# A two-layer decoder step on one core: each weight block multiplied in five matmuls instead of six, the tokens split 286/234 instead of 260/260

## The reference, cut to what matters

```
h = h + rmsnorm(mixer(rmsnorm(h)))
u = rmsnorm(h) @ w_up                     # 1024 x 5632
c = conv_b + u[t-2]*w0 + u[t-1]*w1 + u[t]*w2
h = h + rmsnorm((silu(c[:2816]) * c[2816:]) @ w_down)
h = h + sigmoid(rmsnorm(h) @ w_gate) * (p @ w_proj)
```

## Time and profile before

| | |
|---|---|
| median of 3 runs | 1551.48 us (1548.21 to 1552.59) |
| span of the profiled execution | 1546.4 us, 27972 instructions |
| matmul instructions | 11049, of which 9648 in `product` |
| TensorE busy | 93% of the span |
| VectorE busy | 59% |
| ScalarE busy | 33% |
| DMA | 129.91 MB, mean 84 GB/s |

### The profile page before, as it was taken

The page is one execution under the profiler, slowest core; times in us unless marked ns, Lnnn a source line. Parts: engine busy times, 40 slices in busy tenths (PEclk is TensorE's granted clock), DMA queues, the critical chain, the costliest instruction groups (busy, mean ns, idle before and its releaser), DMA issues.

```text
span 1546.4 us, 27972 instructions
## 1 busy us (share of the span) xinstructions
PE 1433.8 (93%) x11049; PEld 1353.1 (88%) x11049; DVE 909.3 (59%) x1457; ACT 507.8 (33%) x804; POOL 79.6 (5%) x85
## 2 busy tenths in 40 slices
PE   6989998979999999999698988896999999999797
PEld 6989854869999999999698966696999999999787
DVE  4345443568777776322885565747777777522473
ACT  5121130234443443222422134624434434311241
POOL 2000100020000000000400010003000000000110
PEclk9999999889999999999899987998999999999899
DMA  6222510112222223222322220021222222322211
GB/s 206 95 68 84 202 69 14 61 60 69 84 92 95 89 87 111 91 93 90 115 82 71 78 86 1 1 82 32 91 95 83 93 95 89 111 94 93 82 51 72
DMA packets 32643, 129.91 MB, mean 84 GB/s; under 512 B 3961, under 2 KB 4049, under 8 KB 32065
## 3 DMA queue, kind: packets, MB, share of 16 engines
q1 hardware_dynamic: 27792, 110.36, 21.9%
q0 software_dynamic: 4800, 18.86, 3.5%
HBM read 120.57 MB, written 10.04 MB: 84 GB/s over the span
## 4 chain that ended last, share of the span: by engine, by line
PE 85%; DVE 9%; ACT 2%; POOL 2%; issue 2%; DMA 0%; SPq 0%; ACTq 0%; DVEq 0%
PE tile L689 74%; POOL h L357 2%; PE side L729 2%; PE side L862 1%; PE side L959 1%; DVE sm L1532 1%; PE sums L714 1%; DVE cg L1064 1%; PE sums L801 1%; DVE xL L1068 1%; DVE soft L1547 1%; DVE pxL L1068 1%; DVE cv L1079 1%; PE tile L864 1%; PE tile L847 1%
## 5 line engine op out<-in xcount | busy, mean ns | idle before, releaser
L689 PE MATMUL tile<-xH,wH 128*128 128x260 f32 x2256 | 465.1, 287 | 39.9 <-DVE xL L1068 36.1
L455 ACT ACTIVATE wH<-raw 128x1024 fp32r<-128x1024 f32 (+2 forms) x189 | 214.0, 1132 | 766.9 <-PE tile L689 710.9
L689 PE MATMUL tile<-xH,wL 128*128 128x260 f32 x2256 | 457.1, 284 | 0.0
L689 PE MATMUL tile<-xL,wH 128*128 128x260 f32 x2256 | 456.4, 284 | 0.0
L689 PEld LDWEIGHTS tile<-xH,wH 128*128 128x128 f32 x2256 | 352.9, 190 | 49.9 <-issue 37.5
L689 PEld LDWEIGHTS tile<-xH,wL 128*128 128x128 f32 x2256 | 350.3, 190 | 0.0
L689 PEld LDWEIGHTS tile<-xL,wH 128*128 128x128 f32 x2256 | 349.7, 190 | 0.0
L1038 DVE TENSOR_TENSOR wL<-raw,wH 128x1024 fp32r<-128x1024 f32 (+2 forms) x189 | 248.5, 1315 | 162.0 <-ACT wH L455 161.3
L689 PE MATMUL tile<-hidH,wH 128*128 128x260 f32 x704 | 142.1, 283 | 0.1
L689 PE MATMUL tile<-hidH,wL 128*128 128x260 f32 x704 | 141.5, 282 | 0.0
L689 PE MATMUL tile<-hidL,wH 128*128 128x260 f32 x704 | 141.4, 282 | 0.0
(11 more groups left out here) (264 smaller groups left out, 1553.5 us busy)
## 6 DMA issues: line engine op xcount, KB each, us to landing
raw<-in_w_up SPq DMA_DIRECT2D x88, 512.0 KB, 3.3
raw<-in_w_down SPq DMA_DIRECT2D x32, 704.0 KB, 4.0
raw<-in_w_ple SPq DMA_DIRECT2D x16, 640.0 KB, 4.0
raw<-in_w_kv SPq DMA_DIRECT2D x13, 512.0 KB, 3.4
raw<-in_w_qo SPq DMA_DIRECT2D x12, 512.0 KB, 3.3
raw<-in_w_qkv SPq DMA_DIRECT2D x12, 512.0 KB, 3.3
cring<-in_c_in POOLq DMA_DIRECT2D x8, 512.0 KB, 4.9
out_c_s<-cring POOLq DMA_DIRECT2D x8, 512.0 KB, 3.6
```

What stands on the lines that cost most here:

```text
L455: nc.scalar.activation(wH[:, k, 0:n], raw[:, k, 0:n], ACT.Copy).then_inc(s_high, 1)
L689: mm = nc.tensor.matmul(out[:, q, 0:HT], wt[:, s, w], xt[:, k + x[2], q * HT:(q + 1) * HT], start=first and n == 0, stop=last and n == 2)
```

## The change

The tokens are split into A, the first 286, and B, the other 234. The high and low inputs become halves of one tensor (`x2`, `hid2`, `px2`), so that one matmul can stream the B columns of both, 468 columns, against `wH`. The five matmuls of a block are: `wH` with the high A columns, `wH` with the low A columns, `wH` with B high and B low together, `wL` with high A, and `wL` with high B. The A sums lie in the first bank of a tile (columns 226 to 511), the B sums in the second: columns 0 to 233 hold the high part and, added onto it, the `wL` product, columns 234 to 467 the cross term with the low input. Someone must add the two halves of B.

ScalarE does the first half of that: `cross_read` copies the cross columns from PSUM to the new tile `cross`. VectorE then reads a tile in three instructions in place of one (A times `rstd`, B plus `cross`, that sum times `rstd`), or in two in place of one in `copied`. ScalarE's squares in mout, down and sout are now taken from `y`, after VectorE's copy, no longer from PSUM. The small embedding products keep six matmuls, at the widths 286 and 234. The F32 matmuls of the squares keep 260.

```diff
+TA = 286
+TB = T - TA
+B0 = 512 - TA
...
+            def cross_read(stage, st):
+
+                if stage[:4] == "down":
+                    if st.k % 2 == 0:
+                        return
+                    o, k = st.pair, st.k // 2
+                else:
+                    o, k = st.at, st.k
+                act.wait_ge(s_mm, st.at(CHUNK0[stage] + 1))
+                if TILE0[stage] + k >= 2:
+                    act.wait_ge(s_read, o(TILE0[stage] - 1))
+                j = pslot(stage, k)
+                nc.scalar.activation(cross[:, j, :], tile[j][:, 1, TB:2 * TB], ACT.Copy).then_inc(s_cross, 1)
+
             def stream(stage, peel, read, ahead=2):
                 def at_window(st):
+                    cross_read(stage, st + -1)
...
                     if last:
-                        act.wait_ge(s_mm, CHUNK0[stage] + COUNT[stage])
+                        act.wait_ge(s_read, TILE0[stage] + KT)
...
-                    nc.scalar.activation(halves(sq[:, k % 2, :]), tile[pslot(stage, k)][:, :, 0:HT],
+                    nc.scalar.activation(sq[:, k % 2, :], y[:, bass.ds(o(), 1), :].rearrange("p o t -> p (o t)"),
                                          ACT.Square).then_inc(s_last if last else s_read, 1)
...
-                for n, (wt, xt) in enumerate(((wH, x[0]), (wH, x[1]), (wL, x[0]))):
-                    for q in range(2):
-                        mm = nc.tensor.matmul(out[:, q, 0:HT], wt[:, s, w], xt[:, k + x[2], q * HT:(q + 1) * HT],
-                                              start=first and n == 0, stop=last and n == 2)
+                wh, wl, x2k = wH[:, s, w], wL[:, s, w], x[0][:, :, k + x[1], :]
+                a, b = out[:, 0, B0:512], out[:, 1, 0:2 * TB].rearrange("p (c t) -> p c t", c=2)
+                nc.tensor.matmul(a, wh, x2k[:, 0, 0:TA], start=first, stop=False)
+                nc.tensor.matmul(a, wh, x2k[:, 1, 0:TA], start=False, stop=False)
+                nc.tensor.matmul(b, wh, x2k[:, :, TA:T], start=first, stop=last, skip_group_check=True)
+                nc.tensor.matmul(a, wl, x2k[:, 0, 0:TA], start=False, stop=last)
+                return nc.tensor.matmul(b[:, 0], wl, x2k[:, 0, TA:T], start=False, stop=last, skip_group_check=True)
...
             def scaled_read(stage, st, dst, rows=P):
 
                 dve.wait_ge(s_mm, st.at(CHUNK0[stage] + 1))
-                nc.vector.tensor_tensor(halves(dst), tile[pslot(stage, st.k)][0:rows, :, 0:HT],
-                                        halves(rstd[0:rows, :]), ALU.mult).then_inc(s_read, 1)
+                j = pslot(stage, st.k)
+                nc.vector.tensor_tensor(dst[:, 0:TA], tile[j][0:rows, 0, B0:512], rstd[0:rows, 0:TA], ALU.mult)
+                dve.wait_ge(s_cross, st.at(TILE0[stage] + 1))
+                nc.vector.tensor_tensor(dst[:, TA:T], tile[j][0:rows, 1, 0:TB], cross[0:rows, j, :], ALU.add
+                                        ).then_inc(s_sum, 1)
+                dve.wait_ge(s_sum, st.at(SUM0[stage] + 1))
+                nc.vector.tensor_tensor(dst[:, TA:T], dst[:, TA:T], rstd[0:rows, TA:T], ALU.mult).then_inc(s_read, 1)
                 dve.wait_ge(s_read, st.at(TILE0[stage] + 1))
...
-                        if is_last(st):
-                            dve.wait_ge(s_last, sorted(COPIED.values()).index(COPIED[stage]) + 1)
-                        nc.vector.tensor_scalar(
-                            y[:, bass.ds(o(), 1), :].rearrange("p o (q t) -> p (o q) t", q=2),
-                            tile[pslot(stage, k)][:, :, 0:HT], 1.0, None, ALU.mult).then_inc(s_read if is_last(st) else s_yc, 1)
+                        j, yt = pslot(stage, k), y[:, bass.ds(o(), 1), :].rearrange("p o t -> p (o t)")
+                        nc.vector.tensor_scalar(yt[:, 0:TA], tile[j][:, 0, B0:512], 1.0, None, ALU.mult)
+                        dve.wait_ge(s_cross, o(TILE0[stage] + 1))
+                        nc.vector.tensor_tensor(yt[:, TA:T], tile[j][:, 1, 0:TB], cross[:, j, :], ALU.add
+                                                ).then_inc(s_read if is_last(st) else s_yc, 1)
```

More of the change, by code:

```diff
@@ L57 @@
 ON_DVE = {"mout": 0, "down0": KT, "qkv": 2 * KT, "sout": 3 * KT + 1, "down1": 4 * KT + 1}
+SUM0 = {s: TILE0[s] - KT * sum(c[:4] == "down" or c in ("mout", "sout") for c in ORDER[:ORDER.index(s)])
+        for s in ORDER}
 COPIED = {s: (KT - 1) * i for i, s in enumerate(["mout", "down0", "sout", "down1"])}
@@ L157, in build @@
         h = sb("h", [P, KT, T])
-        xH = sb("xH", [P, KT, T], F32R)
-        xL_at = sb.top
-        xL = sb("xL", [P, KT, T], F32R)
+        xL_at = sb.top + size([P, KT, T])
+        x2 = sb("x2", [P, 2, KT, T], F32R)
+        xH, xL = x2[:, 0], x2[:, 1]
         raw = sb("raw", [P, 2, KMAX * P])
@@ L496, in inputs, with squares @@
                     nc.scalar.activation(sq[:, k % 2, :], h[:, k, :], ACT.Square).then_inc(s_sq, 1)
-            def squares(stage, by):
+            def squares(stage, y, by):
                 def read(st):
@@ L565, in _, with feed_forward @@
                 nc.scalar.activation(xH[:, k, :], o_tile(k), ACT.Copy).then_inc(s_xh, 1)
-            def feed_forward(layer, mixer, sqs):
+            def feed_forward(layer, mixer, y):
                 up, down, ple = f"up{layer}", f"down{layer}", f"ple{layer}"
-                stream(mixer, 2, squares(mixer, 1))
+                stream(mixer, 2, squares(mixer, y, 1))
                 second(up)
@@ L600, in feed_forward @@
                 second(down)
-                stream(down, 2, squares(down, 2))
+                stream(down, 2, squares(down, y_down, 2))
                 second(ple)
@@ L613, in feed_forward @@
                 stream(ple, 2, sigmoid)
-            feed_forward(0, "mout", None)
+            feed_forward(0, "mout", y_ml)
             second("qkv")
@@ L678, in _ @@
             x_high(3)
-            feed_forward(1, "sout", None)
+            feed_forward(1, "sout", y_sw)
         @block.tensor
@@ L686, in product, with side_product @@
                 w = slice(k * P, k * P + P)
-                for n, (wt, xt) in enumerate(((wH, x[0]), (wH, x[1]), (wL, x[0]))):
-                    for q in range(2):
-                        mm = nc.tensor.matmul(out[:, q, 0:HT], wt[:, s, w], xt[:, k + x[2], q * HT:(q + 1) * HT],
-                                              start=first and n == 0, stop=last and n == 2)
+                wh, wl, x2k = wH[:, s, w], wL[:, s, w], x[0][:, :, k + x[1], :]
[5 more added lines that the diff above has]
+                return nc.tensor.matmul(b[:, 0], wl, x2k[:, 0, TA:T], start=False, stop=last, skip_group_check=True)
+            def side_product(wh, wl, xh, xl, first, last):
+                for q, t in enumerate((slice(0, TA), slice(TA, T))):
+                    out = side[:, q, B0:512] if q == 0 else side[:, q, 0:TB]
+                    nc.tensor.matmul(out, wh, xh[:, t], start=first, stop=False)
+                    nc.tensor.matmul(out, wh, xl[:, t], start=False, stop=False)
+                    mm = nc.tensor.matmul(out, wl, xh[:, t], start=False, stop=last)
                 return mm
@@ L702, in chunk @@
                 part = st.k % 2 if down else 0
-                xs = (x[0], x[1], part * DKH) if down else (x[0], x[1], 0)
+                xs = (x, part * DKH) if down else (x, 0)
                 if direct and NORM[stage]:
@@ L726, in chunk @@
                         w = slice((KT + k) * P, (KT + k + 1) * P)
-                        for n, (wt, xt) in enumerate(((wH, pH), (wH, pL), (wL, pH))):
-                            for q in range(2):
-                                mm = nc.tensor.matmul(side[:, q, 0:HT], wt[:, s, w], xt[:, k, q * HT:(q + 1) * HT],
-                                                      start=(k == 0 and n == 0), stop=(k == EKT - 1 and n == 2))
+                        mm = side_product(wH[:, s, w], wL[:, s, w], pH[:, k, :], pL[:, k, :], k == 0, k == EKT - 1)
                 mm.then_inc(s_mm, 1)
@@ L1152, in kv_then @@
                                                           op1=ALU.subtract))
-                chain.link(nc.vector.tensor_tensor_scan(out=brow[:], data0=ones[0:NH, 0:1].to_broadcast([NH, SEQ]),
+                chain.link(nc.vector.tensor_tensor_scan(out=brow, data0=ones[0:NH, 0:1].to_broadcast([NH, SEQ]),
                                                         data1=fg[:, 0:SEQ], initial=0.0, op0=ALU.mult, op1=ALU.add))
-                chain.link(nc.vector.tensor_tensor(ig[:, 0:SEQ], ig[:, 0:SEQ], brow[:], ALU.subtract))
+                chain.link(nc.vector.tensor_tensor(ig[:, 0:SEQ], ig[:, 0:SEQ], brow, ALU.subtract))
                 chain.link(nc.vector.tensor_tensor_scan(out=mrow[:], data0=ig[:, 0:SEQ], data1=ig[:, 0:SEQ],
                                                         initial=0.0, op0=ALU.max, op1=ALU.max))
-                chain.link(nc.vector.tensor_tensor(brow[:], brow[:], mrow[:], ALU.add))
+                chain.link(nc.vector.tensor_tensor(brow, brow, mrow[:], ALU.add))
```

28 lines of the change are left out of this document (16 added, 12 removed).

## The result

The changed kernel takes 1572.61 us (median of 4 runs, 1571.77 to 1576.44), the kernel before 1552.03 us on the same chip (4 runs, 1548.21 to 1555.82). The ratio is 1.0136, with a 95% interval of 1.0113 to 1.0158. The forecast was 1498 us, so sign and size are both wrong. Of the executions profiled, before spans 1546.4 us and after 1570.2; before's profiled one was the lowest of its runs (1548.21, 1.8 us above its span), so 3 us of these 23.8 are scatter, and I account for the 20.6 us of the medians.

What follows compares the result with a forecast made beforehand. TensorE was taken as the bound, each matmul costing the longer of its columns and a load floor of some 120 ns. 62.2 us saved less 8.6 uncovered gives 53.6 off 1551.5: 1498 us, range 1484 to 1532.

Steps and rivals of the forecast that it cites:

- What bounds the kernel: Whole kernel: TensorE is the bound, busy 93% of the span, with `product` alone 74% of the chain that ended last.
- the 12 ns: TensorE's product matmuls: time beyond 260 columns' 108.3 ns, read as a weight-load floor of some 120 ns beside the stream.
- the 62.2 us of gain: Product blocks: five matmuls instead of six save 39.7 ns in each of 1568 blocks; bounds 71.3 and 46.1 us.
- The half clock: Start of ple0: at 1.2 GHz 260 columns take 217.5 ns without extra, taken as evidence against a constant cost.
- A floor beside the stream: Every product matmul: takes the longer of its columns and its weight load's floor, some 120 ns with F32R columns.
- a constant per matmul: Rival, chance 0.06: each product matmul costs 12 ns over its columns at any width; kernel at 1541 us.
- The other rivals: 234 columns leave the fast rate, 1974 us (0.08); 468 stream slower, 1662 (0.03); VectorE bounds up, 1526 (0.08).
- VectorE's reads and ScalarE's copy: Tile reads: 0.70 to 1.26 us, copy 0.38, `wL` 1.47 us after the read; covered by TensorE's next chunk.
- Where nothing covers it: Stage ends, third up chunks and directly taken tiles: the longer reads cost 8.6 us together.
- The ends of mout, down and sout: Last tile's square waits for copy, VectorE's add and hand-overs: 0.84 us, four times, 3.4 us.
- The third chunks of up0 and up1: Late read: 0.32 us of gain lost and the read 0.56 longer, 0.88 twice, 1.8 us.
- The six reads of 0.56 us: kv's first and last tiles, the last of qo, ple0, qkv and ple1: 0.56 us each, 3.4 us.

Runs made afterwards that it cites:

- the series: Kernel before with 16 back-to-back matmuls of each kind appended behind its last stage, only their distances counted; F32R: 260 columns 119 ns, 234 columns 111 ns.
- the old reads: Kernel before with six matmuls of 286 and 234 columns, one VectorE read per tile, no ScalarE copy: 1578.22 us, ratio 1.0172.
- the new: Changed kernel with the 468-column matmul cut into two of 234, copy and three reads kept: 1585.36 us, 1.0209 times before.
- 264/256: Changed kernel with the tokens split 264/256, so the joint matmul has 512 columns: 1561.06 us, ratio 1.0050 to before.
- 280/240: Changed kernel with the tokens split 280/240, so the joint matmul has 480 columns: 1558.82 us, ratio 1.0043 to before.
- the five with the new reads: Changed kernel and its four variants (six matmuls, 264/256, 280/240, 468 columns from one run), all with copy and split reads: 1572.61, 1585.36, 1561.06, 1558.82, 1565.26 us.

## Why the prediction was wrong

**What bounds the kernel** held: TensorE is the bound before and after, and no engine took its place.

**The step that failed** is the reading of the 12 ns: "What vanishes when the stream gets slower is a floor, something that goes on beside the stream and takes about 120 ns; the weight load of each matmul is the candidate." Two inferences were wrong in it. The load's floor is 109 ns and lies under the stream of 260 columns: halving the load changed nothing there. And wider matmuls don't absorb the excess: it is 10 to 16 ns at all widths from 234 to 512, where the forecast had it gone at 286 (0 to 2 ns) and at 468 (2 ns). By the series, a block costs three of 286 at 129 to 133, one of 468 at 219 and one of 234 at 111: 717 to 729, against six of 260 at 119 to 120, 714 to 720. TensorE alone measured 724 and 719. Of the 62.2 us of gain nothing came, and 12.3 us of loss stood in its place.

**The half clock** The earlier trace rows was read rightly as a row and wrongly as an argument. After, the start of ple0 shows columns at 1.2 GHz and no excess again, at all widths: 0.39 us for 468, 0.24 for 286, 0.20 for 234.

```profile
757.52 0.59 PE L717 MATMUL tile<-px,wH 128*128 128x468 f32 x1
757.91 0.44 PE L718 MATMUL tile<-px,wL 128*128 128x286 f32 x1
758.15 0.40 PE L719 MATMUL tile<-px,wL 128*128 128x234 f32 x1
758.35 0.66 PE L751 MATMUL sums<-sq,const 128*128 128x260 f32 x1
```

So an excess that is there at full clock for every width vanishes at half clock for every width. A floor beside the stream was one explanation of its vanishing, not the only one. And the prediction's own rows spoke against it: the earlier trace rows have the load at half clock, 218 ns for each plain F32 matmul of 8 columns with its load of 128, where the series of 128 columns have 109 ns at full clock. By these numbers the load slows down with the clock as the stream does. A floor of 120 ns at full clock would then be some 240 ns at half clock (an estimate), over the 217.5 that the earlier trace rows show. What makes the excess, and makes it vanish, no run here shows; it goes with the type, since bf16 has 2.5 to 3.3 ns of it. The Trainium skill (TensorE: Matmul & The Clock Gate, "Wait — 56ns, not 53.3ns?") describes just such a cost: some 2.5 ns of each matmul, whatever its width, that show only at 2.4 GHz. The bf16 series agree, with 2.5 to 3.3 ns; for F32R it has no figure, and the series give 10 to 16. The rule itself spoke against the sentence "A constant cost of a matmul would still be there".

**The rival "a constant per matmul"** named nearly the right prices for two of the three widths, 131, 207 and 110; measured were 129 to 133, 215 to 219 and 111. It got 0.06 for the half clock's sake. It too would have had the wrong sign (1541): it took the excess of the wide matmul for 12 ns, where it is 16 in one run and 20 to 24 as the kernel reads it. That is what eats the 12 ns of the matmul saved: six matmuls to five gave 6.7 ns a block, while the split 286/234 cost 17 with the old reads and 15 with the new (738.0 and 735.5 against 720.7). The joint matmul needs only that B has at most 256 columns: at 264/256 and 280/240 the block of five was 4.5 and 2.1 ns under that of before, and the kernels were still slower, by what lies outside the blocks. The other rivals did not come: 234 columns stay at the fast rate, 468 cost 0.22 us and not 0.30, and VectorE still waits for TensorE in up0.

**VectorE's reads and ScalarE's copy** were priced rightly. After, VectorE's timeline of one window of up0:

```profile
405.60 0.46 DVE L1124 TENSOR_TENSOR u<-tile,rstd 128x286 f32<-128x286 f32 x1 [0.79 <-PE tile L719]
406.08 0.40 DVE L1126 TENSOR_TENSOR u<-tile,cross 128x234 f32<-128x234 f32 x1
406.51 0.40 DVE L1129 TENSOR_TENSOR u<-u,rstd 128x234 f32<-128x234 f32 x1
407.04 1.23 DVE L1072 TENSOR_TENSOR wL<-raw,wH 128x1024 fp32r<-128x1024 f32 x1
```

0.46 + 0.40 + 0.40 = 1.26 us as forecast, and `wL` starts 1.44 us after the read, where 1.47 was said and the earlier trace rows have 1.09. TensorE's block did not shrink, so 0.79 us of waiting is left here instead of 0.13. As long as a chunk lasts 5.8 us the edit costs nothing in this loop.

**Where nothing covers it**, 8.6 us were forecast; the account has 8.3 for this kernel, and TensorE's idle time grew by 10.0 here and by 9 on average over the five with the new reads. That the total came out so near is in part luck, since not every term was right. The ends of mout, down and sout were right in size, forecast at 0.84 us each: the view of waits has 0.7 for each. ScalarE's timeline at the end of down0, which answers to the earlier trace rows:

```profile
744.28 0.37 ACT L480 ACTIVATE cross<-tile 128x234 f32<-128x234 f32 x1 [6.67 <-PE tile L719]
745.11 0.64 ACT L538 ACTIVATE sq<-y_down 128x520 f32<-128x520 f32 x1 [0.47 <-DVE y_down L1147]
```

The square starts 0.83 us after the tile is there, 0.37 of copy and 0.47 of waiting for VectorE's sum. Before, it started at once. The third chunks of up0 and up1 were placed rightly: TensorE waits up to 0.5 us for `u`, where the longer read was priced at 0.56. Missed were longer waits for `wL`, 3.7 us before and 5.5 after; the two in kv grew by 0.4 us each. The six reads of 0.56 us where the next work takes a tile directly were not measured one by one.

## What to carry to other kernels

Before merging matmuls, measure the cost of one at the widths that come out of it, not only at the one in use: sixteen of a kind behind the kernel tell it in a microsecond or four, and here they would have refused the change. Where two explanations fit one number, look for the row that varies the suspected cause itself (a smaller load, a wider stream), not one that varies everything at once, as the clock does. And a change that splits the reading of a result pays at the starts and ends of stages, where no next chunk covers it: here some 9 us, more than the best split won in the blocks (6.3).

## What the runs showed of the hardware

- An F32R matmul at full clock takes columns/2.4 and 10 to 16 ns, at 234 to 512 columns; bf16 takes 2.5 to 3.3 ns over its columns; at half clock F32R has no excess (217.5 ns for 260 columns, 390 for 468). Why stays open.
- The load of 128 columns of 4-byte weights limits a matmul at 109 ns; with 64 columns of weights the same 128 columns of stream take 60 ns. At half clock plain F32 matmuls of 8 columns, each with a load of 128, start 218 ns apart. In bf16, 128 columns of weights and 128 of stream take some 56 ns, an estimate from the 1.06 us of their row, less some 0.22 for one matmul, over 15.
- Six matmuls of 286 and 234 columns take 736 ns and six of 260 take 719, with the same number of columns. Single series explain a part of it, 720 to 732 with 286 at 129 to 133; that alternating the widths adds the rest is likely and not shown. Moving the split by 6 tokens, to 280/240, gave 10 ns a block, of which the series give 6 to the start of the two runs (213 ns from column 280, 219 from 286). Why the start matters, and only with the runs four rows apart, stays open.
- Changing between F32R and bf16 and back costs some 18 ns (a block of 720 ns where the series give 702). Grouped by type, the same matmuls made the kernel 0.6% faster.
